# Fewer products, fewer splits and a twelve-part last load in the expert stage of a decoder layer on one Trainium2 core

## The chip, the cores and the metric

The kernel runs on one core of one Trainium2 chip. The metric is device time in microseconds (us) of one execution. Lower is better.

## The reference, cut to what matters

The layer has two parts: a mixer (convolution, sparse attention, retention), which the change leaves alone, and a mixture of 32 experts with top-4 routing over N = 320 tokens of width 1024, in fp32:

```
gate, top_e = softmax(top4(h @ w_router + b_router))       # 4 experts for each token
hu  = x @ w_up[e] + b_up[e]                                # 1024 -> 2048
g   = minimum(hu[:, 0::2], 7.0)
u   = clip(hu[:, 1::2], -7.0, 7.0)
act = (u + 1.0) * g * sigmoid(1.702 * g)
y_e = act @ w_down[e] + b_down[e]                          # 1024 -> 1024
y   = LN(alpha * h + sum_k gate_k * y_k + per_layer_embedding)
```

The 1280 pairs of token and expert make about 40 rows an expert. All weights of all experts are read once: 32 x 12 MB.

## The kernel before, in words

**The stage of the experts.** One *item* is up to 128 rows (slots) of one expert. Item i gathers its rows from `h_dram` (POOL, L1936), turns them (`turn_x`, PE, L536), makes the up product, turns the result back (`turn_hidden`), applies the gated activation, makes the down product and scatters the rows to `y_dram` (POOL, L1942). With these inputs there are 32 items. An item with more than 64 rows is called *many* here (`many_i` holds the flag); there are five, and 27 *few* items.

**Weights.** A weight matrix comes in 1 MB chunks of 128 x 2048: eight for up, four for down, 12 an item (`PER`). SP issues the loads in order (`next_weights`, L465), each into one of six buffers (`chunk_in`) when VectorE has split the chunk that was there (`lo_ready`). The products run in the one-pass fp32r format, so each chunk is split in two: ScalarE writes the rounded part `w_hi` (L1205, waits for the load `w_here` and for `chunk_used`, PE's count of finished chunks), and VectorE writes the rest `w_lo = chunk - w_hi` (L1743, waits for `hi_ready`). Both are rings of three.

**Products.** A *few* item packs its up operand: columns 0:64 of `x_hi` hold the rounded rows and columns 64:128 their rest, so that two passes (`x_hi w_hi`, `x_hi w_lo`) do what a *many* item does in three. `turn_hidden` multiplies with a matrix `turner` that is set for each item (L1758) and adds the two halves for a few item. A many item turns in two halves, and the second waits until VectorE has read the first out of the same two banks (`turned_read`). The down product has three passes for every item: 4 chunks x 3 passes x 4 products = 48.

**Order on PE.** `item(i)`: `turn_hidden(i)`, up product of i+1, `turn_x(i+2)`, down product of i. In ScalarE's and VectorE's order, written out by hand, `part(t)` is one chunk: t = 0 to 7 is the up product of i+1, t = 8 to 11 the down product of i. Between the parts stand, on ScalarE, `result_copy(i-1)` (L1188) after part 2, `squash` (sigmoid, L1192) after 3, `hidden_high` (L1196) after 4, four `hidden_copy` (L1183) after 9, `rows_copy` (L1163) after 10; on VectorE, `hidden_rows` (L1771 to L1791) after part 2, `hidden_product` (L1799) after 3, `hidden_low` (L1806) after 4, `rows_low` (L1755, or L1752 for many) after 9.

**The end.** When the last scatter has landed, SP loads `y_dram` in four transfers (two of 2 MB, two of 512 KB). VectorE then does three token tiles one after the other: four weighted adds (L1871), LayerNorm with `bn_stats` (L1279 to L1282, ScalarE's square root L1014 between), two passes for gain and bias (L1873, L1874); POOL stores each tile (L1966).

Of the kernel before, what the change touches and what calls it, by code (L numbers as in the profile page):

```python
# [20 lines left out]
CAP = 128  # L21
# [124 lines left out]
def build(nc, A, O):  # L146
# [11 lines left out]
    with ctx:  # L158
# [133 lines left out]
        turner, turn_fold, few, many_f = ec.take(HALF), ec.take(HALF), ec.take(NI + 8), ec.take(NI + 8)  # L292
# [13 lines left out]
        y_rows = y_part[:, 0:D]  # L306
        ple = [y_part[:, 0:D], y_part[:, D:2 * D], uu.rearrange("p a b -> p (a b)")]
        y_tok = [arena[:, 0:2 * SLOT], arena[:, 2 * SLOT:4 * SLOT]]
# [28 lines left out]
        up_done, hu_ready, turner_ready = sem("up_done"), sem("hu_ready"), sem("turner_ready")  # L337
        hu_turned, turned_read, g_ready, e_ready, act_ready = sem("hu_turned"), sem("turned_read"), sem("g_ready"), sem("e_ready"), sem("act_ready")
        bias_hi, bias_ready, gates_hi, gates_ready = sem("bias_hi"), sem("bias_ready"), sem("gates_hi"), sem("gates_ready")
        y_stored, var_ready, std_ready = sem("y_stored"), sem("var_ready"), sem("std_ready")  # L340
        y_ready, y_sent, y_here, y_out = sem("y_ready"), sem("y_sent"), many("y_here", 3), sem("y_out")
# [32 lines left out]
        PER = 12  # L374
# [27 lines left out]
        def _(sp):  # L402
# [77 lines left out]
            def next_weights(s, e, c, buf):  # L480

                sp.wait_ge(lo_ready, s + 1)
                weights_to(e, c, buf)

            def first_loads(r):
                s = r * NE * PER
                for t in range(8):
                    e, c = (0, t + 6) if t < 2 else (1, t - 2)
                    next_weights(s + t, e, c, t % 6)

            def item_loads(i, e):
                s = i * PER + 8
                for t in range(PER):
                    of, c = (e + 1, t + 6) if t < 2 else (e, t + 6) if t < 6 else (e + 2, t - 6)
                    next_weights(s + t, of, c, (8 + t) % 6)

            def last_loads(i):
                s = i * PER + 8
                for t in range(6):
                    of, c = (NE - 1, t + 6) if t < 2 else (NE - 2, t + 6)  # L500
                    next_weights(s + t, of, c, (8 + t) % 6)
                for t in range(6, 10):
                    next_weights(s + t, NE - 1, t + 2, (8 + t) % 6)
# [11 lines left out]
            for r in range(1, ROUNDS):  # L515
                with sp.If(n_items > r * NE):
                    for c in range(6):
                        next_weights(r * NE * PER - 6 + c, 0, c, c)
# [4 lines left out]
            rows = y_dram.rearrange("(t k) d -> t (k d)", k=TOPK)  # L523
# [7 lines left out]
        def _(pe):  # L531
# [372 lines left out]
            def turn_half(rhs, inc):  # L904
                for s in range(2):
                    for j in range(8):
                        cols = hu[:, 2 * j * 128 + s:2 * (j + 1) * 128:2]
                        last = mm(psum[:, 6 + s, j * HALF:(j + 1) * HALF], cols, rhs, True, True)
                last.then_inc(hu_turned, inc)

            def turn_hidden(i, many_slots, x_next):
                pe.wait_ge(hu_ready, i * 4 + 4)
                pe.wait_ge(turner_ready, i + 1)
                pe.wait_ge(xlo_ready, x_next)
                with pe.If(many_slots > 0):
                    turn_half(turner, 1)
                    pe.wait_ge(turned_read, i * 2 + 1)
                    turn_half(ident[:, HALF:CAP], 1)
                with pe.If(many_slots < 1):
                    turn_half(turner, 2)  # L920

            def up_product(i, s, many_slots):
# [4 lines left out]
                def product(passes):  # L927
                    for k in range(KT):
                        pe.wait_ge(hi_ready, s + (k + 1))
                        for n_pass, (x, w) in enumerate(passes):  # L930
                            if w is w_lo:
                                pe.wait_ge(lo_ready, s + (k + 1))
# [17 lines left out]
            def down_product(i, s, first):  # L950
                pe.wait_ge(act_hi_ready, i + 1)
                pe.wait_ge(act_lo_ready, i + 1)
                for q in range(4):
                    at = (first + q) % 3
                    pe.wait_ge(hi_ready, s + (q + 1))
                    for n_pass, (x, w) in enumerate(((act_hi, w_hi), (act_lo, w_hi), (act_hi, w_lo))):
                        if w is w_lo:
                            pe.wait_ge(lo_ready, s + (q + 1))
# [1098 lines left out]
```

## Time and profile before

| | |
|---|---|
| median of 3 runs | 1720.52 us (1718.29 to 1721.14) |
| the profiled execution | 1708.54 us, span 1706.7 us |
| granted TensorE clock, mean | 0.916 |
| stage of the experts | from about 490 us to 1650 us of the span |
| after it | 1650 us to 1706.7 us |
| HBM read, mean over the span | 499.43 MB, 292 GB/s moved |

Busy time is in us; "idle before" is the time that the engine sat idle ahead of the instructions of a row and what released it. In a table of windows each row is one stretch of the span.

### The profile page before, as it was taken

The numbers are of one execution on the slowest core, as the hardware profiler recorded it, in microseconds if no ns is written. First come the engines' busy times: TensorE is split into PE (matmuls) and PEld (weight loads), VectorE is DVE, ScalarE is ACT, GpSimd is POOL, SyncE is SP. The second block draws the span as 40 slices with busy tenths as digits, with TensorE's granted clock in tenths as the row PEclk, the third lists the DMA queues.
The fourth block names the chain that finished last, engine by engine and source line by source line (L and its number), as shares of the span: only waits on it lengthen the run. The fifth ranks groups of instructions, "written<-read, shape, count | busy, mean of one in ns | idle before, by whom it ended". The sixth has DMA issues, their size and how long they took to land.

```text
span 1706.7 us, 22653 instructions
## 1 busy us (share of the span) xinstructions
PE 1470.8 (86%) x6949; PEld 1136.5 (67%) x6950; DVE 1289.7 (76%) x1327; ACT 1007.1 (59%) x878; POOL 306.2 (18%) x416
## 2 busy tenths in 40 slices
PE   6983677899989999999999999999998999999950
PEld 4761566554447777777777777777887778778740
DVE  0246564764568899999799999999878997998836
ACT  0111323510147788887688888788756876887620
POOL 5303988800300100010000100100000010000000
PEclk9995787769888999999899999999988999999875
DMA  9984353151348999999799999999977998899742
GB/s 354 359 244 142 91 203 142 28 192 53 134 189 328 350 387 390 384 393 382 261 384 383 390 384 388 384 383 393 362 271 273 389 393 321 327 391 366 272 148 71
DMA packets 123930, 498.52 MB, mean 292 GB/s; under 512 B 20977, under 2 KB 46146, under 8 KB 89618
## 3 DMA queue, kind: packets, MB, share of 16 engines
q1 hardware_dynamic: 103122, 454.56, 70.4%
q0 software_dynamic: 14768, 29.16, 4.9%
q10 hardware_dynamic: 5984, 14.11, 2.4%
q8 instruction: 28, 0.46, 0.1%
q14 instruction: 28, 0.23, 0.0%
HBM read 499.43 MB, written 26.25 MB: 308 GB/s over the span
## 4 chain that ended last, share of the span: by engine, by line
PE 50%; DVE 18%; issue 13%; ACT 8%; SPq 6%; DMA 5%; DVEq 1%; ACTq 0%; POOL 0%; POOLq 0%
PE psum L533 47%; DVE w_lo L1743 9%; ACT w_hi L1205 5%; SPq L388 4%; PE psum L536 3%; DMA arena<-in_w_up 3%; DMA early<-in_pages 1%; DVE arena L1799 1%; DVE arena L1871 1%; DVE arena L1262 1%; DVE arena L1390 1%; DVE arena L1389 1%; DVE arena L1291 1%; ACT arena L1183 1%; SPq L385 1%
## 5 line engine op out<-in xcount | busy, mean ns | idle before, releaser
L1743 DVE TENSOR_TENSOR w_lo<-arena,w_hi 128x2048 fp32r<-128x2048 f32 x384 | 860.9, 2287 | 53.1 <-ACT w_hi L1205 48.8
L1205 ACT ACTIVATE w_hi<-arena 128x2048 fp32r<-128x2048 f32 x376 | 715.3, 1917 | 235.0 <-PE psum L533 234.4
L533 PE MATMUL psum<-w_hi,x_split 128*128 128x512 f32 x2208 | 580.8, 398 | 11.2 <-DVE x_split L1806 6.1
L533 PEld LDWEIGHTS psum<-w_hi,x_split 128*128 128x128 f32 x2208 | 416.8, 191 | 98.7 <-issue 8.5
L533 PE MATMUL psum<-w_lo,x_split 128*128 128x512 f32 x1536 | 432.8, 404 | 49.6 <-DVE w_lo L1743 44.9
L533 PE MATMUL psum<-arena 128*128 128x64 f32 (+10 forms) x2258 | 398.5, 352 | 50.9 <-DMA arena<-in_w_in 17.0
L533 PEld LDWEIGHTS psum<-arena 128*128 128x128 f32 (+4 forms) x2258 | 316.9, 207 | 134.3 <-issue 76.6
L533 PEld LDWEIGHTS psum<-w_lo,x_split 128*128 128x128 f32 x1536 | 282.4, 191 | 155.0 <-DVE w_lo L1743 101.8
L1942 POOL DMA_INDIRECT y_dram<-y_part,arena x32 | 49.9, 1559 | 1044.0 <-ACT y_part L1188 952.4
L536 PE MATMUL psum<-arena 128*128 128x128 f32 (+4 forms) x501 | 80.2, 312 | 66.5 <-ACT arena L1067 28.9
L536 PEld LDWEIGHTS psum<-arena 128*128 128x128 f32 (+4 forms) x501 | 66.0, 158 | 81.3 <-issue 37.3
L1291 DVE TENSOR_REDUCE arena<-early 128x32 f32<-128x2048 f32 x16 | 35.8, 2281 | 109.4 <-DMA early<-in_pages 109.4
L1898 POOL TENSOR_SCALAR arena<-arena,conv_w 128x256 f32<-128x256 f32 (+1 forms) x120 | 84.5, 704 | 11.8
L1899 POOL TENSOR_TENSOR arena<-arena 128x256 f32<-128x256 f32 (+1 forms) x120 | 68.6, 572 | 10.0
L1183 ACT ACTIVATE arena<-psum 128x512 f32<-128x512 f32 x128 | 65.4, 596 | 4.5 <-PE psum L533 3.9
L533 PE MATMUL psum<-early,arena 128*128 128x512 f32 (+1 forms) x152 | 65.5, 634 | 0.0
L1035 ACT ACTIVATE arena<-psum 128x320 f32<-128x320 f32 x23 | 10.1, 437 | 91.2 <-PE psum L533 90.5
L1936 POOL DMA_INDIRECT arena<-h_dram,arena x32 | 39.0, 1219 | 69.2 <-PE psum L536 55.6
L1262 DVE COPY arena<-psum 128x128 f32<-128x128 f32 (+5 forms) x62 | 26.2, 435 | 32.7 <-PE psum L536 21.1
L533 PEld LDWEIGHTS psum<-early,arena 128*128 128x128 f32 (+1 forms) x152 | 25.0, 178 | 37.5 <-issue 37.4
L1755 DVE TENSOR_TENSOR x_split<-psum,x_split 128x512 fp32r<-128x512 f32 x27 | 18.7, 692 | 38.0 <-ACT x_split L1163 36.9
L1019 ACT ACTIVATE arena<-psum 128x512 f32<-128x512 f32 (+6 forms) x32 | 15.9, 517 | 52.0 <-PE psum L536 51.9
(216 smaller groups left out, 758.8 us busy)
## 6 DMA issues: line engine op xcount, KB each, us to landing
arena<-in_w_up SPq DMA_DIRECT2D x256, 1024.0 KB, 7.3
arena<-in_w_down SPq DMA_DIRECT2D x128, 1024.0 KB, 6.9
early<-in_pages SPq DMA_DIRECT2D x160, 128.0 KB, 2.6
arena<-in_w_in ACTq DMA_DIRECT2D x23, 512.0 KB, 7.3
arena<-in_pages POOLq DMA_DIRECT2D x32, 128.0 KB, 7.9
early<-in_pages POOLq DMA_DIRECT2D x32, 128.0 KB, 6.6
arena<-in_pages SPq DMA_DIRECT2D x32, 128.0 KB, 2.2
early<-in_w_plg SPq DMA_DIRECT2D x1, 4096.0 KB, 14.7
```

Of the source, the lines that this page charges most:

```text
L388: eng.dma_start(dst[:, bass.ds(k * 1024 + n * 256, 256)], A["pages"][bass.ds(page, 1), :, part * 256:part * 256 + 256].rearrange("a p n -> ...
L533: return TE.matmul(out, lhsT, rhs, start=start, stop=stop, skip_group_check=True)
L536: return TE.transpose(out, in_, ident[0:in_.shape[0], 0:in_.shape[0]])
L1183: SE.activation(hu[0:CAP, n * 512:n * 512 + 512], psum[0:CAP, n, :], ACT.Copy).then_inc(hu_ready, 1)
L1205: SE.activation(w_hi[:, (8 + t) % 3], chunk_in[(8 + t) % 6], ACT.Copy).then_inc(hi_ready, 1)
L1262: last = VE.tensor_copy(dst, src)
L1291: last = VE.tensor_reduce(cm[:, b, kind].rearrange("p (a b) -> p a b", b=2), cmp_slot[:, b % 2, :, kind].rearrange("p a (b s) -> p a b s", ...
L1743: VE.tensor_tensor(w_lo[:, at], chunk_in[buf], w_hi[:, at].bitcast(f32), SUB).then_inc(lo_ready, 1)
L1898: seen(GE.tensor_scalar(tmp, src(t), conv_w[:, k, t:t + 1], None, MUL))
L1899: seen(GE.tensor_tensor(dst, dst, tmp, ADD))
L1936: pool.indirect_dma_start(out=xg, out_offset=None, in_=h_dram, in_offset=bass.IndirectOffsetOnAxis(ap=slots[:, i, 0:1].bitcast(u32), axis= ...
L1942: pool.indirect_dma_start(out=y_dram, out_offset=bass.IndirectOffsetOnAxis(ap=slots[:, i, 1:2].bitcast(u32), axis=0), in_=y_rows, in_offse ...
```

## The change

Four things change.

1. **Down product of a few item packed.** `hidden_low` writes the rest of the activation into columns 64:128 of `act_hi`, and the product has two passes instead of three. The result stands in two halves of partitions: ScalarE copies the lower half out (`y_low`), and VectorE adds (`result_sum`, new, in VectorE's order after part 2 of the next item). For a many item ScalarE copies the two banks in two instructions. `turner` is gone: a few item turns with a fixed `folder`. The second half of a many item's turn goes to banks 4 and 5, and waits for `y_ready` of the item before instead of `turned_read`. ScalarE branches on `many` too.
2. **The last of the four down chunks is not split.** PE multiplies it straight in fp32 from the load's buffer, 4 products (`act_sb`, `raw`). There are 11 splits an item (`SPLIT`). SP frees that buffer on PE's `chunk_used`, not on `lo_ready`.
3. **Silu.** `act_sb = Silu(1.702 g)` on ScalarE; VectorE then forms `(u + 1) * act_sb` in one instruction, and L1786/L1788/L1791 go. The factor 1.702 is taken out of the gates (`g4`).
4. **The end.** Twelve loads of `y_dram`, one for each tile and choice, each with its own semaphore. The moments are taken on ScalarE (`accum_out`), the order is weigh 0, weigh 1, normalize 0, weigh 2, normalize 1, normalize 2, and a tile's normalization is three VectorE instructions.

```diff
 def next_weights(i, t, e, c, buf, last=False):
+    if t == (3 if last else 11):
+        sp.wait_ge(chunk_used, i * PER + (8 + t + 1 + 3))
+    else:
+        sp.wait_ge(lo_ready, i * SPLIT + (8 + t + 1))
     weights_to(e, c, buf)
...
 def turn_hidden(i, many_slots, x_next, begin):
     with pe.If(many_slots > 0):
+        turn_half(ident[:, 0:HALF], 6).then_inc(hu_turned, 1)
+        if not begin:
+            pe.wait_ge(y_ready, i)
+        turn_half(ident[:, HALF:CAP], 4).then_inc(hu_turned, 1)
     with pe.If(many_slots < 1):
+        turn_half(folder, 6).then_inc(hu_turned, 2)
...
+def down_product(i, first, many_slots):
...
+    def product(passes, rows):
+        for q in range(3):
...
+        pe.wait_ge(w_here[buf], i * 32 + ((first + 3) // 6 * 16 + 16))
+        for a, c in ((0, 0), (0, 1), (1, 0), (1, 1)):
+            last = mm(psum[0:rows, 4 + c, :], act_sb[:, 6 + a, 0:rows], raw[:, a * D + c * 512:a * D + c * 512 + 512], False, a == 1)
         last.then_inc(chunk_used, 1)
+    with pe.If(many_slots > 0):
+        product(((act_hi, w_hi), (act_lo, w_hi), (act_hi, w_lo)), CAP)
+    with pe.If(many_slots < 1):
+        product(((act_hi, w_hi), (act_hi, w_lo)), HALF)
...
 def result_copy(i, used, many_slots):              # ScalarE
+    with act.If(many_slots > 0):
+        SE.activation(y_rows[:, 0:512], psum[:, 4, :], ACT.Copy).then_inc(y_half, 1)
+        SE.activation(y_rows[:, 512:D], psum[:, 5, :], ACT.Copy).then_inc(y_ready, 1)
+    with act.If(many_slots < 1):
+        SE.activation(y_low..., psum[HALF:CAP, 4:6, :], ACT.Copy).then_inc(y_half, 1)
 def squash(i, many_slots):
+    with act.If(many_slots > 0):
+        SE.activation(act_sb, gg, ACT.Silu, scale=SALPHA).then_inc(e_ready, 1)
+    with act.If(many_slots < 1):
+        SE.activation(act_sb[:, :, 0:HALF], gg[:, :, 0:HALF], ACT.Silu, scale=SALPHA).then_inc(e_ready, 1)
...
+def result_sum(i, many_slots):                     # VectorE
+    with dve.If(many_slots < 1):
+        dve.wait_ge(y_half, i + 1)
+        VE.tensor_tensor(y_rows[0:HALF]..., psum[0:HALF, 4:6, :], y_low..., ADD).then_inc(y_ready, 1)
...
-sp.dma_start(y_tok[0], rows[0:128]).then_inc(y_here[0], 16)
-sp.dma_start(y_tok[1], rows[128:256]).then_inc(y_here[1], 16)
-for n in range(2):
-    sp.dma_start(chunk_in[4 + n][0:64], rows[256:320, n * SLOT:(n + 1) * SLOT]).then_inc(y_here[2], 16)
+for m in range(3):
+    for k in range(TOPK):
+        sp.dma_start(y_tok[m][k], rows[m * 128:m * 128 + MT[m], k]).then_inc(y_here[m * TOPK + k], 16)
...
+act.wait_ge(sum_ready, m + 1)                      # ScalarE, for m in range(3)
+SE.activation(spare, acc[0:M, m], ACT.Copy, scale=-1.0 / D, accum_out=mean).then_inc(y_mean, 1)
+SE.activation(spare, acc[0:M, m], ACT.Square, bias=mean, accum_out=y_sq[0:M, m:m + 1]).then_inc(square_ready, 1)
+act.wait_ge(var2_ready, m + 1)
+SE.activation(y_std[0:M, m:m + 1], y_sq[0:M, m:m + 1], ACT.Sqrt).then_inc(std2_ready, 1)
```

VectorE also clears `act_sb` and the upper half of `y_rows` once ahead of the stage, and the set-up of `turn_fold` and `few` is gone.

## Rows read from the trace of the kernel before

**Rows 1.** The page's busy time by engine: busy us, share, instructions.
```profile
PE 1470.8 (86%) x6949; PEld 1136.5 (67%) x6950; DVE 1289.7 (76%) x1327; ACT 1007.1 (59%) x878; POOL 306.2 (18%) x416
```

**Rows 2.** Windows as long as one item: busy by engine, clock, DMA share, GB/s.
```profile
593.15:626.30 33.15, 31.39 (x154) 25.23 (x153) 31.26 (x22) 28.10 (x20) 2.80 (x3) 1.00 1.00 392
...
825.20:858.35 33.15, 28.80 (x134) 24.00 (x133) 24.66 (x22) 18.16 (x12) 2.72 (x2) 0.85 0.70 250
858.35:891.50 33.15, 31.38 (x154) 25.24 (x153) 31.26 (x22) 28.11 (x21) 2.82 (x2) 1.00 1.00 380
...
1488.20:1521.35 33.15, 31.38 (x154) 25.23 (x153) 31.24 (x22) 28.08 (x21) 2.80 (x2) 1.00 1.01 405
```

**Rows 3.** The chain that ended last, in order of time: start, us, what.
```profile
611.24 16.54 PE psum L533 x88
...
644.39 16.54 PE psum L533 x88
...
859.11 16.54 PE psum L533 x88
```

**Rows 4.** Who waited for whom, 560 to 1706 us: total, times, longest.
```profile
ACT w_hi L1205 <- PE psum L533: 226.0, 167, 14.1
...
PE psum L533 <- DVE w_lo L1743: 42.7, 50, 1.2
```

**Rows 5.** The weight loads of L465, 560 to 1600 us, issue to landing.
```profile
DMA to landing us min/median/max: 4.8/7.3/10.9
```

**Rows 6.** VectorE's timeline, one few item: start, duration, instruction.
```profile
681.11 0.69 DVE L1755 TENSOR_TENSOR x_split<-psum,x_split 128x512 fp32r<-128x512 f32 x1 [1.09 <-ACT x_split L1163]
681.72 11.09 DVE L1743 TENSOR_TENSOR w_lo<-arena,w_hi 128x2048 fp32r<-128x2048 f32 x5
692.72 0.69 DVE L1771 TENSOR_TENSOR arena<-psum,arena 128x512 f32<-128x512 f32 x1
...
694.87 0.69 DVE L1791 SCALAR_TENSOR_TENSOR arena<-arena 128x512 f32<-128x512 f32 x1 [0.19 <-DVE arena L1778]
696.04 2.29 DVE L1743 TENSOR_TENSOR w_lo<-arena,w_hi 128x2048 fp32r<-128x2048 f32 x1 [0.48 <-ACT w_hi L1205]
```

**Rows 7.** ScalarE's timeline, the same item.
```profile
694.09 1.92 ACT L1205 ACTIVATE w_hi<-arena 128x2048 fp32r<-128x2048 f32 x1 [2.79 <-PE psum L533]
```

**Rows 8.** PE's timeline around the first many item.
```profile
791.90 2.10 PE L533 MATMUL psum<-w_hi,x_split 128*128 128x512 f32 x8
...
813.80 1.04 PE L536 MATMUL psum<-arena 128*128 128x128 f32 x8
...
825.57 3.87 PE L533 MATMUL psum<-arena 128*128 128x64 f32 x32
831.26 6.85 PE L533 MATMUL psum<-arena 128*128 128x64 f32 x32 [1.82 <-DVE arena L1772]
...
869.86 0.34 PE L533 MATMUL psum<-arena 128*128 128x64 f32 x2
```

**Rows 9.** Windows: fp32 products of 512 columns, and the clock.
```profile
832.00:833.00 1.00, 1.00 (x7) 1.00 (x6) 0.60 (x1) 0.00 (x0) 0.42 (x1) 0.50 0.97 344
841.00:842.00 1.00, 1.00 (x4) 0.81 (x3) 0.00 (x0) 0.34 (x1) 0.00 (x0) 0.59 0.00 0
...
440.00:448.00 8.00, 8.00 (x20) 3.58 (x19) 2.90 (x4) 0.60 (x1) 5.96 (x6) 1.00 0.05 7
```

**Rows 10.** The timeline of the end.
```profile
1649.07 1.02 ACT L1188 ACTIVATE y_part<-psum 128x1024 f32<-128x1024 f32 x1 [6.21 <-PE psum L533]
...
1654.19 0.36 SPq L524 DMA_DIRECT2D arena<-y_dram  x1
...
1655.37 1.28 ACT L1014 ACT_TABLE_LOAD   x1 [5.28 <-issue]
...
1662.37 5.25 DVE L1871 SCALAR_TENSOR_TENSOR arena<-arena 128x1024 f32<-128x1024 f32 x4 [17.18 <-DMA arena<-y_dram]
...
1695.19 0.55 POOL L1966 DMA_DIRECT2D out_y<-arena  x1 [10.19 <-DVE arena L1874]
```

More of the change, by code:

```diff
@@ L291, in build @@
         stats2, mv2, rstd2 = ec.take(2, 6), ec.take(2), ec.take(1)
-        turner, turn_fold, few, many_f = ec.take(HALF), ec.take(HALF), ec.take(NI + 8), ec.take(NI + 8)
+        y_sum, y_mu, y_sq, y_std = ec.take(3), ec.take(3), ec.take(3), ec.take(3)
+        folder, many_f = ec.take(HALF), ec.take(NI + 8)
         ln2 = split(hu, (2, D))
@@ L975, in item @@
                     pe.wait_ge(y_ready, i)
[L976 removed]
+                down_product(i, 16 if end < NE else 8, here)
             def stream(r):
@@ L1183, in hidden_copy @@
                     SE.activation(hu[0:CAP, n * 512:n * 512 + 512], psum[0:CAP, n, :], ACT.Copy).then_inc(hu_ready, 1)
-            def result_copy(i, used):
-                act.wait_ge(chunk_used, used + 3)
-                act.wait_ge(y_sent, i * 16 + 16)
-                SE.activation(y_rows.rearrange("p (c n) -> p c n", c=2), psum[:, 4:6, :], ACT.Copy).then_inc(y_ready, 1)
-            def squash(i):
-                act.wait_ge(g_ready, i + 1)
-                SE.activation(act_sb, gg, ACT.Sigmoid, scale=SALPHA).then_inc(e_ready, 1)
@@ new lines, in squash, with hidden_high @@
+            def squash(i, many_slots):
+                with act.If(many_slots > 0):
+                    act.wait_ge(g_ready, i + 1)
+                    SE.activation(act_sb, gg, ACT.Silu, scale=SALPHA).then_inc(e_ready, 1)
+                with act.If(many_slots < 1):
+                    act.wait_ge(g_ready, i + 1)
+                    SE.activation(act_sb[:, :, 0:HALF], gg[:, :, 0:HALF], ACT.Silu, scale=SALPHA).then_inc(e_ready, 1)
+            def hidden_high(i, many_slots):
+                with act.If(many_slots > 0):
+                    act.wait_ge(act_ready, i + 1)
+                    SE.activation(act_hi, act_sb, ACT.Copy).then_inc(act_hi_ready, 1)
+                with act.If(many_slots < 1):
+                    act.wait_ge(act_ready, i + 1)
+                    SE.activation(act_hi[:, :, 0:HALF], act_sb[:, :, 0:HALF], ACT.Copy).then_inc(act_hi_ready, 1)
@@ L1226, in item @@
                     rows_copy(i + 2)
-                part(11)
             def stream(r):
@@ L1813, in part @@
                 def part(t):
-                    low(s + t, (8 + t) % 3, (8 + t) % 6)
+                    low(i * SPLIT + (8 + t), (8 + t) % 3, (8 + t) % 6)
                 for t in range(3):
                     part(t)
+                if not begin:
+                    result_sum(i - 1, is_many(i - 1))
                 hidden_rows(i, e, here)
@@ L1821, in item @@
                     hidden_low(i, here)
-                    part(3)
+                    result_sum(i, here)
                     return
@@ L1827, in item @@
                 hidden_low(i, here)
-                for t in range(5, 8):
+                for t in range(5, 11):
                     part(t)
-                set_turner(i + 1)
-                part(8)
-                part(9)
                 if end < NE - 1:
                     rows_low(i + 2, is_many(i + 2))
-                part(10)
-                part(11)
             def stream(r):
```

214 lines of the change are left out of this document (115 added, 99 removed).

## The prediction

> **What bounds the kernel now.** I read the page first: PE is busy 86% of the span and VectorE 76% [rows 1]. That is a mean over two different parts, so I cut the experts' stage into windows of one item. In a few item PE is busy 31.4 us of 33.15, VectorE 31.3, ScalarE 28.1, and the DMA engines are at a share of 1.00 with 392 GB/s [rows 2]. Three resources stand within 6% of the period, and the question is which one sets it.
>
> The chain repeats every 33.15 us (611.24 to 644.39) [rows 3], to a few hundredths. Two rows say that this period is VectorE's. ScalarE waited 226.0 us for PE to free `w_hi`, and no wait of it for a load is among the long ones [rows 4]. And after a many item, when all six buffers have had time to fill (share 0.70 in that window), the next item still takes 33.15 us [rows 2, 3]: a kernel bound by its loads would have caught up. VectorE's timeline has hardly a gap in it: five `w_lo` back to back in 11.09 us, 2.22 us each, then the hidden rows; idle are 1.09, 0.19 and 0.48 us [rows 6], which with the 31.3 us busy makes 33.1.
>
> The second row of importance is the share of the DMA engines. When it is 0.70 the rate is 250 GB/s; at 1.00 it is 380 to 405 [rows 2]. The rate divided by the share is 357 to 401, so the share is a fair measure of capacity, and a few item already uses about 99% of it. Its load is 12 MB (12.58 million bytes) and about 0.25 million of gather and scatter: 12.83 million at 390 GB/s are 32.9 us, at 405 they are 31.7.
>
> A many item is bound by PE: its up product alone takes from 791.90 to 813.80, 21.9 us, and its turn 3.87 + 1.82 idle + 6.85, the last at half clock [rows 8, 9]. The two intervals around it last 37.4 and 44.3 us (from 788.1, which is the first product less a turn of 3.87, to 825.57, then to 869.86) [rows 8].
>
> Counting the steady intervals between many items gives 20; the other intervals of the stage touch a many item, its start or its end.
>
> **The change, part by part.**
>
> *VectorE in a few item.* Gone: one `w_lo` (2.22), `turner` (64 columns, an estimate of 0.2, well below the 0.69 of 512 columns), L1791 (0.61 of pitch and 0.19 idle), and the 1.09 of waiting ahead of `rows_low`, because `rows_low` now stands after the last split, in the shadow of the unsplit product [rows 6]. Added: `result_sum`, 1024 columns from PSUM: between 0.69 for 512 columns and 2.29 for 2048, in proportion 1.22 (ends 0.7 and 2.3). Net -2.2-0.8-0.2-1.1+1.2 = -3.1 before new waits.
>
> *PE in a few item.* Down goes from 48 one-pass products to 24 plus 4 in fp32. The 48 take from 814.6 (`turn_x` begins at 813.80 and takes 0.8) to 825.57, 0.228 each [rows 8]. Fp32: 16 products of a turn are recorded as x32 [rows 8], so a product is two records; 20 records of 512 columns filled 8.00 us [rows 9], 0.80 a product. So 24 x 0.228 + 4 x 0.80 = 8.7 instead of 10.9: -2.2. For many it is 36 x 0.228 + 3.2 = 11.4: +0.5.
>
> *ScalarE in a few item.* One `w_hi` less (1.92 [rows 7]), Silu and `hidden_high` on half the columns (512 fewer each, a quarter of 1.92, so -0.45 each): -2.8. It has five us of idle already and decides nothing.
>
> *The new critical loop.* I follow it from the start of the last split, at 0. `w_lo` ends at 2.2; PE's last pass 1.1; the fp32 products 3.2; so the raw chunk is released at 6.6. Only then may ScalarE start the third `w_hi` of the next item (its slot is counted behind that chunk): 8.6. VectorE has done `rows_low` and two splits by 7.6, waits 1.0, then third split 10.8, `result_sum` 12.0, hidden rows 14.0. The fourth `w_hi` needs the turn (3.87) and PE's first chunk (1.8): ready 14.4, so the fourth split ends 16.6; product 17.3, split 19.5, `hidden_low` 20.2, and the last of the next six splits of 2.2, where the loop closes, starts at 31.2. That is the period by compute alone, 31.2; with small new branches and register loads I take 31.6. It is 1.5 below today's, but the loads need 31.7 to 32.9.
>
> *SP.* The raw chunk's buffer comes free 4.4 us later than a split would free it, and two loads queue behind it on SP. With a landing time of 7.3 us at the median [rows 5] and 2.7 us a load, two to three loads are outstanding, so the DMA engines do not run dry in that pause once they are the bound.
>
> (If they did run dry there, the pause of 4.4 us less the 2.7 to 5 that is outstanding would cost up to 1.7 an interval, and the 33.15 of today would come back; that is the last rival.) So steady intervals go from 33.15 to between 31.6 (right after a many item, when buffers are full) and 32.9. The mean I take is 32.5: 20 x 0.65 = **-13**. Ends: 31.6 everywhere, -31; the old 33.15, 0.
>
> *Around many items.* The interval with a many up product and a few down product is PE's: -2.2 each, four of them, -9. The interval with the many turn gains 0.5 for the product and loses about as much in VectorE's shorter rows: 0. The turn's gap stays: `y_ready` now comes after the third split and the sum, 5.5 us after the down product's end, while the first half takes 3.87, so 1.6 to 1.9 us of gap against 1.82 [rows 8], and the fall of the clock to 0.50 until 841.6 [rows 9] stays with it. Only where one many item follows another is no sum in the way, and the gap goes: 1.8, and up to 5 with its stretch of half clock; I take 2. Together **-11** (ends -4 and -16).
>
> *Last item.* From the hidden rows to the last copy: down product -2.2, half-width Silu and `hidden_high` -0.9, L1791 -0.6, sum +1.2: **-2**.
>
> *The end.* Now the first add starts 8.2 us after the issue of the loads (1654.19 to 1662.37), and the three tiles take 32.8 us up to POOL's store at 1695.19 [rows 10]. With a load of 512 KB at about 370 GB/s, 1.4 us each, the first should land after some 3.7 us (its 2 MB forerunner: 8.2, of which 5.6 is transfer). Eight adds of 1.31 are then paced by the landings: 3.7 + 7 x 1.4 + 1.3 = 14.8. Then normalize 0 (variance, wait for Sqrt, reciprocal, two passes of 1.3): 3.3; four adds 5.2; normalize 1, 3.4; normalize 2, with ScalarE's two passes just in time, 3.6: 30.3 against 41.0. **-10** (ends -7 and -12). The extra clears ahead of the stage fall in an idle stretch of VectorE: 0.
>
> Sum: -13 - 11 - 2 - 10 = -36. The profiled execution is 1708.54 us (span 1706.7 and 1.8 around it), 12.0 below the median of 1720.52; I put the difference on the median: 1684.5, **1685 us**.
>
> **Rivals.**
>
> *The table of Silu is loaded in each item.* The trace before has no load in the items' loop, where Copy and Sigmoid alternate; a change of table costs 1.28 us where it occurs [rows 10]. Silu now stands in branches, so what is loaded when they join may be unknown. One load lies between the fourth `w_hi` and Silu and delays the fifth by about 1.0: a compute period of 32.6, which eats what there was after many items: steady 20 x (33.15 - 32.8) = -7, sum -30, 1691. Two loads: 33.9, +15, sum -8, 1713. Centre 1702. Nothing in the rows decides whether it happens.
> "ScalarE activation tables: per-element evaluation and per-set limits" in the Trainium skill (Table sets in the compiler and the runtime) says that the compiler places the loads block by block. "ScalarE: Activation LUTs" (What ACT_TABLE_LOAD costs) adds a drain of about 1.38 us to the 1.28 that the trace shows; by that, an estimate, the loop would be 34.0 us and the result 1715, still not slower.
>
> *The loads are not the bound.* Then 31.6 holds throughout: -31 - 16 - 2 - 12, 1660. For it: 405 GB/s over one item [rows 2]. Against: shares of 1.00 at 380 and 392.
>
> *The clock falls in few items: the case on the other side.* PE will idle some 4 us an item, up to 1.9 at once ahead of the fourth chunk, where VectorE now does the sum as well. Today the longest wait for `w_lo` is 1.2 us [rows 4] at full clock, and after the gap of 1.82 ahead of a turn it fell to 0.50 for ten us [rows 8, 9]. If it falls in each few item, the turn costs 2.98 more and the first chunk 1.8: 31.6 + 4.5 = 36.1, 20 x 3 = +60, 1757. It decides against the change from a steady interval of 34.3 on (23 us spent). Against it: the new gaps stand between products of 512 columns, not beside the turn.
>
> *Nothing gained in steady items* (the new wait for the sum or for the raw chunk gives 33.1 again): only -11 - 2 - 10, 1697.
>
> **How the numbers follow.** Chances: forecast 0.45, no bound by loads 0.12, Silu's tables 0.20, nothing gained when steady 0.13, clock 0.10. The range takes in all but part of the first rival's two-load end, the extreme of the second and the clock: 1662 to 1709. What a measurement can tell from no change is 0.2%, 3.4 us. All cases but the clock and a corner of the tables are faster: faster 0.87, same 0.03, slower 0.10.
>
> **What would show it.** Spacing of steady items 31.6 to 32.9 with the DMA share at 1.00 and ScalarE now waiting for loads; two passes in L533's chunks of the down product and about 3.2 us of fp32 ahead of the turn; no table load between the items; the gap in a many turn still there and one less; the first weighted add some 4 us after the first load's issue and the last store about 30 us after it. Wrong would make it: steady items at 33.1 or above, a granted clock under 1.00 in them, or table loads in the loop.

## The result and the profile after

The changed kernel takes 1742.05 us at the median (8 runs, 1730.35 to 1747.28), the kernel before on the same chip 1720.55 us (8 runs). The ratio is 1.0124 (95% interval 1.0097 to 1.0151): slower by 1.2%, 21.5 us, where 36 us less were forecast. It is above the range, and the profiled execution takes 1745.72 us with a span of 1744.1. One execution of the kernel of experiment 4, of nine, took 2917.53 us, in a slow state, and is left out of its ratio.

The head of the page, busy time of each engine (against [rows 1]):

```profile
span 1744.1 us, 22207 instructions
PE 1473.8 (85%) x6497; PEld 1069.8 (61%) x6498; DVE 1216.5 (70%) x1243; ACT 1024.5 (59%) x930; POOL 290.2 (17%) x416
```

VectorE and PE have less to do, as they should, and the span is longer. So what has grown is the waiting, and the place is found by the groups by line. On ScalarE there are three that the loop did not have before (instructions, then busy us and mean ns of one, then idle us before them):

```profile
L1244 ACT ACT_TABLE_LOAD x31 | 39.8, 1283 | 0.6
L1227 ACT ACT_TABLE_LOAD x27 | 34.6, 1283 | 0.5
L1224 ACT ACT_TABLE_LOAD x5 | 6.4, 1283 | 0.1
```

L1224 and L1227 are Silu in its two branches, L1244 is the `w_hi` behind it, a Copy. Together that is a table load ahead of Silu and another one right behind it, in practically every item. ScalarE's timeline shows them in one item (start, duration, instruction, and in brackets the idle time before it):

```profile
711.11 1.92 ACT L1244 ACTIVATE w_hi<-arena 128x2048 fp32r<-128x2048 f32 x1 [2.86 <-PE psum L537]
713.05 1.28 ACT L1227 ACT_TABLE_LOAD   x1
714.34 0.63 ACT L1227 ACTIVATE arena<-arena 128x512 f32<-128x512 f32 x1
714.99 1.28 ACT L1244 ACT_TABLE_LOAD   x1
716.29 1.91 ACT L1244 ACTIVATE w_hi<-arena 128x2048 fp32r<-128x2048 f32 x1
```

Between the fourth `w_hi` and the fifth there are 3.26 us, of which 2.56 are loads. VectorE and PE are behind it and have nothing else to do. VectorE's timeline, the same item:

```profile
718.23 2.29 DVE L1791 TENSOR_TENSOR w_lo<-arena,w_hi 128x2048 fp32r<-128x2048 f32 x1 [2.27 <-ACT w_hi L1244]
```

and PE's:

```profile
718.25 1.20 PE L537 MATMUL psum<-w_hi,x_split 128*128 128x512 f32 x4 [1.67 <-ACT w_hi L1244]
720.58 2.08 PE L537 MATMUL psum<-w_lo,x_split 128*128 128x512 f32 x4 [1.13 <-DVE w_lo L1791]
722.45 1.72 PE L537 MATMUL psum<-w_hi,x_split 128*128 128x512 f32 x4
```

Four products take 2.08 us instead of 1.08: they run at half clock. The windows of 1 us say so (busy us of PE, PE's weight loads, VectorE, ScalarE, GpSimd; then granted clock, share of the DMA engines, GB/s):

```profile
720.00:721.00 1.00, 0.42 (x1) 0.42 (x2) 1.00 (x2) 1.00 (x2) 0.00 (x0) 0.70 0.85 348
721.00:722.00 1.00, 1.00 (x3) 0.74 (x3) 1.00 (x2) 1.00 (x1) 0.00 (x0) 0.50 0.93 217
722.00:723.00 1.00, 1.00 (x4) 0.78 (x3) 1.00 (x1) 0.63 (x2) 0.00 (x0) 0.50 0.67 197
723.00:724.00 1.00, 1.00 (x4) 0.77 (x3) 1.00 (x2) 1.00 (x1) 0.00 (x0) 0.59 1.01 406
724.00:725.00 1.00, 1.00 (x6) 0.81 (x5) 1.00 (x1) 0.61 (x1) 0.00 (x0) 1.00 1.28 422
```

0.50 is the lower of TensorE's two levels, 1.2 GHz, and it comes after 1.67 and 1.13 us of idle PE with 1.2 us of work between them. The same two gaps do not bring it each time. PE two items earlier, and the window of that item:

```profile
648.94 1.19 PE L537 MATMUL psum<-w_hi,x_split 128*128 128x512 f32 x4 [1.65 <-ACT w_hi L1244]
651.27 1.19 PE L537 MATMUL psum<-w_lo,x_split 128*128 128x512 f32 x4 [1.14 <-DVE w_lo L1791]
```

```profile
631.16:665.71 34.55, 30.33 (x136) 21.51 (x136) 29.46 (x20) 28.21 (x22) 2.21 (x2) 1.00 0.92 344
```

Of the 14 steady items that the chain shows, 3 have a granted clock of 1.00 and take 34.51 to 34.55 us, 7 have 0.95 and take 34.53 to 34.78, 4 have 0.90 or 0.91 and take 35.91 to 36.06. Why the clock falls in some of them and not in others stays open. The chain gives the spacing of the items, against 33.15 in [rows 3]:

```profile
595.10 10.60 PE psum L537 x52
631.16 10.62 PE psum L537 x52
665.71 10.60 PE psum L537 x52
700.49 10.60 PE psum L537 x52
```

36.06, 34.55, 34.78. From 560.37 to 771.17 six of them average 35.13, from 922.08 to 1201.70 eight average 34.95: 35.03 together, 1.88 more than before. With some 20 such intervals that is +38 us. The experts' stage (first `w_hi` to the start of the last scatter) went from 1161.5 to 1194.5 us, +33.0; what follows the last scatter's start from 55.8 to 48.6.

The end came out much as forecast. The issue of the loads (SP) and what follows, against [rows 10]:

```profile
1699.39 6.65 SPq L531 DMA_DIRECT2D arena<-y_dram  x12
```

```profile
1703.65 2.67 DVE L1910 SCALAR_TENSOR_TENSOR arena<-arena 128x1024 f32<-128x1024 f32 x2 [8.88 <-DMA arena<-y_dram]
1716.49 1.28 DVE L1910 SCALAR_TENSOR_TENSOR arena<-arena 128x1024 f32<-128x1024 f32 x1 [2.25 <-DMA arena<-y_dram]
```

```profile
1732.57 0.55 POOL L2028 DMA_DIRECT2D out_y<-arena  x1 [2.55 <-DVE arena L1926]
```

The first add comes 4.26 us after the issue (3.7 forecast) and the last store 33.2 us after it, against 41.0.

### The profile page after: what moved, and what is told of

The parts are those of the page before. It is cut to its first block, busy times and chain, and to the rows that moved or that the text cites. A ratio compares the mean times of both kernels' runs of the same rounds, so it can differ in the third digit from the quotient of the medians.

```text
span 1744.1 us, 22207 instructions
## 1 busy us (share of the span) xinstructions
PE 1473.8 (85%) x6497; PEld 1069.8 (61%) x6498; DVE 1216.5 (70%) x1243; ACT 1024.5 (59%) x930; POOL 290.2 (17%) x416
## 4 chain that ended last, share of the span: by engine, by line
PE 49%; DVE 16%; ACT 13%; issue 12%; SPq 6%; DMA 2%; ACTq 1%; DVEq 0%; POOL 0%; POOLq 0%
PE psum L537 47%; DVE w_lo L1791 9%; ACT w_hi L1244 6%; SPq L391 4%; PE psum L540 2%; ACT arena L1204 2%; ACT L1244 2%; ACT arena L1227 1%; DMA early<-in_pages 1%; DMA arena<-y_dram 1%; DVE arena L1435 1%; DVE arena L1434 1%; DVE arena L1336 1%; SPq L388 0%; ACT arena L1082 0%
## 5 line engine op out<-in xcount | busy, mean ns | idle before, releaser
L1791 DVE TENSOR_TENSOR w_lo<-arena,w_hi 128x2048 fp32r<-128x2048 f32 x352 | 794.6, 2289 | 198.1 <-ACT w_hi L1244 197.4
L1244 ACT ACTIVATE w_hi<-arena 128x2048 fp32r<-128x2048 f32 x344 | 653.1, 1915 | 260.4 <-PE psum L537 259.6
L537 PE MATMUL psum<-arena 128*128 128x64 f32 (+8 forms) x2514 | 521.1, 382 | 47.6 <-DMA arena<-in_w_in 17.0
L537 PE MATMUL psum<-w_hi,x_split 128*128 128x512 f32 x1628 | 462.6, 414 | 53.6 <-ACT w_hi L1244 44.5
L537 PEld LDWEIGHTS psum<-arena 128*128 128x128 f32 (+3 forms) x2514 | 356.8, 205 | 215.2 <-issue 162.8
L537 PE MATMUL psum<-w_lo,x_split 128*128 128x512 f32 x1408 | 419.5, 422 | 53.0 <-DVE w_lo L1791 51.1
L537 PEld LDWEIGHTS psum<-w_hi,x_split 128*128 128x128 f32 x1628 | 318.3, 200 | 132.3 <-ACT w_hi L1244 55.8
L2004 POOL DMA_INDIRECT y_dram<-y_part,arena x32 | 39.0, 1219 | 1092.0 <-DVE y_part L1851 788.1
L540 PEld LDWEIGHTS psum<-arena 128*128 128x128 f32 (+4 forms) x501 | 66.2, 158 | 79.1 <-issue 37.6
L1851 DVE TENSOR_TENSOR y_part<-psum,y_part 64x1024 f32<-64x1024 f32 x27 | 32.6, 1208 | 13.7 <-ACT y_part L1219 13.7
```

The costliest lines, as they stand in the source:

```text
L537: return TE.matmul(out, lhsT, rhs, start=start, stop=stop, skip_group_check=True)
L540: return TE.transpose(out, in_, ident[0:in_.shape[0], 0:in_.shape[0]])
L1244: SE.activation(w_hi[:, (8 + t) % 3], chunk_in[(8 + t) % 6], ACT.Copy).then_inc(hi_ready, 1)
L1791: VE.tensor_tensor(w_lo[:, at], chunk_in[buf], w_hi[:, at].bitcast(f32), SUB).then_inc(lo_ready, 1)
L1851: VE.tensor_tensor(y_rows[0:HALF].rearrange("p (c n) -> p c n", c=2), psum[0:HALF, 4:6, :], y_low.rearrange("p (c n) -> p c n", c=2), ADD) ...
L2004: pool.indirect_dma_start(out=y_dram, out_offset=bass.IndirectOffsetOnAxis(ap=slots[:, i, 1:2].bitcast(u32), axis=0), in_=y_rows, in_offse ...
```

## The experiments

Times of the kernel before beside the experiments are 1718.1 to 1721.0 us. Each ratio is against it.

**1. Sigmoid back, all else as changed.**

```diff
-  SE.activation(act_sb, gg, ACT.Silu, scale=SALPHA)        # in both branches
+  SE.activation(act_sb, gg, ACT.Sigmoid, scale=SALPHA)
+  VE.scalar_tensor_tensor(out=u, in0=u, scalar=1.0, in1=g, op0=ADD, op1=MUL)
-  VE.tensor_scalar(g4, g4, 1.0 / SALPHA, None, MUL)
```

> The changed kernel with one part undone: sigmoid and the multiplication by g on VectorE are back (L1786/L1791 of before), all else as changed, the branches on ScalarE too. Theory T (the two table loads of 1.28 us around Silu delay the fifth w_hi by about 2.6, and the gap of 1.67 + 1.13 us that this opens on PE lets the clock fall to 0.50 for some 3 us): no table load in the items, granted clock near 1.00 in few items, steady items 31.8 to 32.9 us instead of 34.7, time near 1685 to 1695. Rival U (the unsplit chunk or the sum after the third split is what makes the loop longer): steady items stay at 34 or above and the time at 1735 or above. Rival J (the branch alone, without Silu, makes the back end load a table): table loads still there, 2.6 us an item, time as changed or above.

1679.07 us, ratio 0.9758 (0.9745 to 0.9770), below the 1685 to 1695 expected, and no table load between items. The branches are the same: Sigmoid in them needs no load. All of the loss, and 42 us beyond it, goes with Silu.

**2. Silu alone in the kernel before, in straight code** (with what follows from it on VectorE, part 3 of the change).

```diff
-  SE.activation(act_sb, gg, ACT.Sigmoid, scale=SALPHA).then_inc(e_ready, 1)
+  SE.activation(act_sb, gg, ACT.Silu, scale=SALPHA).then_inc(e_ready, 1)
```

> The kernel before with Silu alone: ScalarE's squash is Silu on all columns in straight code, without a branch, and VectorE's L1786 to L1791 go. Theory T-join (loads come from branches, after which the loaded table is not known): no table load in the loop, VectorE 0.8 us shorter, steady items 32.4 to 32.9 instead of 33.15, time 1703 to 1718. Rival S (Silu's table and the one that Copy is given are two, whatever the flow): two loads an item, steady items about 33.15 - 0.8 + 2.3 = 34.7, time near 1755.

1720.18 us, ratio 0.9993 (0.9965 to 1.0020). One load, at the first use of Silu in the whole stage:

```profile
L1192 ACT ACT_TABLE_LOAD x1 | 1.3, 1283 | 0.0
```

So Silu and Copy go together without loads. A second reading: the steady items stay at 33.17 us (chain, 590.74 to 623.91), though L1791 is gone and VectorE is busy for 30.56 us in each instead of 31.26 [rows 2]. VectorE's work did not set the 33.15, and the 1703 to 1718 expected, which rested on it, was missed.

**3. The changed kernel with Silu unbranched.**

```diff
-  with act.If(many_slots > 0):
-      SE.activation(act_sb, gg, ACT.Silu, ...)
-  with act.If(many_slots < 1):
-      SE.activation(act_sb[:, :, 0:HALF], gg[:, :, 0:HALF], ACT.Silu, ...)
+  SE.activation(act_sb, gg, ACT.Silu, scale=SALPHA).then_inc(e_ready, 1)
```

> The changed kernel with Silu on all columns outside of the branch; hidden_high and result_copy keep their branches. T-join: no table load in the items, steady items 31.8 to 32.9, time 1683 to 1695. Rival S: two loads an item as in the changed kernel, time 1740 to 1745.

**1672.72 us, ratio 0.9726 (0.9706 to 0.9746)**: the fastest of all, 48 us below the kernel before and below the 1683 to 1695 expected. Silu takes 1.04 us for all columns instead of 0.63, and yet it is far ahead, because both loads are gone. ScalarE's timeline at the same place in an item:

```profile
637.18 1.92 ACT L1240 ACTIVATE w_hi<-arena 128x2048 fp32r<-128x2048 f32 x1 [2.86 <-PE psum L537]
639.01 1.04 ACT L1223 ACTIVATE arena<-arena 128x1024 f32<-128x1024 f32 x1
639.96 1.90 ACT L1240 ACTIVATE w_hi<-arena 128x2048 fp32r<-128x2048 f32 x1
```

Its windows of two steady items (columns as above):

```profile
594.40:626.56 32.16, 30.00 (x136) 21.59 (x136) 29.46 (x20) 26.70 (x20) 2.19 (x2) 1.00 0.98 384
626.56:658.72 32.16, 29.99 (x137) 21.60 (x137) 29.47 (x20) 26.30 (x20) 2.22 (x2) 1.00 1.01 402
```

The steady items take 32.16 us at full clock, all but one of 33.54 (from 560.86). In that second window the share of the DMA engines is 1.01 at 402 GB/s; before it was 1.00 at 392 [rows 2].

**4. The end alone, in the kernel before** (twelve loads of `y_dram`, moments on ScalarE, the new order; nothing else).

> The kernel before with the end of the change alone (twelve loads, moments on ScalarE, three VectorE instructions a tile). From the changed kernel's trace: first add 4.3 us after the first load's issue, last store 33.2 us after it, against 41.0 before. All theories: 7 to 8 us faster, 1711 to 1714. If the end gained nothing, 1720.

1715.45 us, ratio 0.9968 (0.9944 to 0.9993), 5 us by the medians where 7 to 8 were expected. In its trace the last store is 32.8 us after the issue of the loads, 8.2 less than before.

**5. Packing undone, in the third kernel.**

```diff
-  product(((act_hi, w_hi), (act_hi, w_lo)), HALF)
+  product(((act_hi, w_hi), (act_lo, w_hi), (act_hi, w_lo)), HALF)
# and no result_sum, no y_low; hidden_high on all columns
```

> e3_silu_unbranched with three passes in a few item's down product, no sum on VectorE, one copy out on ScalarE and hidden_high on all columns; the fourth chunk stays unsplit. Theory (PE's down product lies in the loop): 12 products more, 2.7 us, of which part is hidden behind the splits: steady items 33.2 to 34.5, time 1692 to 1715. Rival (VectorE's total work sets the period, and the sum of 1.2 goes): steady items near 31.0 to 32.2, time 1650 to 1673.

1709.14 us, ratio 0.9918 (0.9884 to 0.9951). The chain gives 34.21 us:

```profile
590.42 17.59 PE psum L537 x84
624.63 17.59 PE psum L537 x84
```

VectorE has less to do here than with packing (no sum of 1.21 us), and the item is 2.05 us longer. PE is busy 2.5 us longer in it, for 12 products; ScalarE rounds the activation on twice the columns, some 0.4 us. So most of the 2.05 is PE's down product, and the loop runs through it.

**6. The fourth chunk split again, in the third kernel.**

```diff
-  PER, SPLIT = 12, 11
+  PER, SPLIT = 12, 12
-  for q in range(3):
+  for q in range(4):
-  for a, c in ((0, 0), (0, 1), (1, 0), (1, 1)):    # fp32 from raw
```

> e3_silu_unbranched with the fourth down chunk split like the others (12 splits, part 11 back, two passes for few and three for many). Theory (the loop runs through PE's down product, turn and first up chunk and not through VectorE's sum of work; a split of 2.2 us instead of 3.2 us of fp32 leaves the loop as long): steady items 32.2 to 32.8, time 1673 to 1690. Rival (VectorE's total work sets the period): 32.16 + 2.2 = 34.4, time 1720.

1697.84 us, ratio 0.9882 (0.9816 to 0.9947), 25 us above the third kernel and above the 1673 to 1690 expected. Where the clock holds the item is even shorter: 31.81 us where the third kernel has 32.04 at the same place behind a many item, and 31.97 for the next (to 956.70) against 32.16, with VectorE busy nearly all the time; VectorE's timeline, one item apart:

```profile
892.92 2.29 DVE L1782 TENSOR_TENSOR w_lo<-arena,w_hi 128x2048 fp32r<-128x2048 f32 x1 [1.46 <-ACT w_hi L1233]
924.73 2.29 DVE L1782 TENSOR_TENSOR w_lo<-arena,w_hi 128x2048 fp32r<-128x2048 f32 x1
```

But the clock does not hold everywhere. Windows of 100 us:

```profile
600.00:700.00 100.00, 91.40 (x399) 71.22 (x398) 91.50 (x60) 80.31 (x60) 8.29 (x6) 0.91 0.95 372
900.00:1000.00 100.00, 89.30 (x422) 68.40 (x422) 98.44 (x63) 86.69 (x63) 11.42 (x6) 1.00 0.99 397
```

So the unsplit chunk does not pay by a shorter loop. What goes with the 25 us is the clock: with that chunk every steady item of the third kernel's trace is at 1.00, and without it, of five in a row from 588.32 on, one stands at 0.90 (34.69 us), two at 0.86 (36.08 and 35.91 us) and two at 1.00 (32.0 us). Why it falls there was not tested.

**7. Branches around Silu, in the second kernel,** and the load of `many` into a register that they need. Both branches do the full columns, so that the work is the same.

```diff
-  SE.activation(act_sb, gg, ACT.Silu, ...)
+  with act.If(many_slots > 0):  SE.activation(act_sb, gg, ACT.Silu, ...)
+  with act.If(many_slots < 1):  SE.activation(act_sb, gg, ACT.Silu, ...)
```

> e2_silu_alone (no loads in the loop, steady items 33.17 us, 1720 us) with Silu put into a branch on many, on all columns either way, and nothing else. T-join (after a branch the loaded table is not known, so Silu and the Copy behind it each get a load): two loads an item, steady items 35.3 to 36.0, time 1765 to 1785. Rival (the loads of the changed kernel needed its other branches, of hidden_high and result_copy, too): no loads, 1720.

1798.85 us, ratio 1.0461 (1.0402 to 1.0521), above what either theory gave; the steady items take 36.1 us on average of 13, a little above the 36.0 expected, and where the rest of the excess lies stays open. The loads are there again:

```profile
L1210 ACT ACT_TABLE_LOAD x31 | 39.8, 1283 | 0.6
L1197 ACT ACT_TABLE_LOAD x27 | 34.6, 1283 | 0.5
L1194 ACT ACT_TABLE_LOAD x5 | 6.4, 1283 | 0.1
```

It takes Silu and the branch together: Silu in straight code has no loads (experiment 2), and Sigmoid in branches has none either (experiment 1). They are as many, 32 and 31, as in the changed kernel. Why the compiler gives them to Silu and not to Sigmoid stays open.

**8. Loads in place without a branch, in the third kernel.**

```diff
+  SE.activation(y_std[0:1, 0:1], many_f[0:1, 0:1], ACT.Sqrt)        # one element, ahead of Silu
   SE.activation(act_sb, gg, ACT.Silu, scale=SALPHA)
```

> e3_silu_unbranched with a Sqrt on one element right ahead of Silu, so that the same two loads stand where the changed kernel has them, without a branch. If the loads at that place are the whole loss: steady items 34.7 to 35.5, clock falling to 0.50 for some 3 us in many of the few items, time 1735 to 1755. Rival (the branch itself costs, in fetching or in its waits): steady items near 33, time under 1715.

1766.87 us, ratio 1.0285 (1.0236 to 1.0334), above the 1735 to 1755 expected. Sqrt and Silu each load a table (2 x 1.28, and 0.2 for the element); steady items take 36.41 and 35.28 us in turn, 35.83 on average of six (chain, 559.79 to 774.79). Two loads alone, put back at this place, turn the fastest kernel into one slower than before.

**9. Copies in place of the loads.** Six copies of one element ahead of Silu and six behind it, no load.

> The kernel with Silu unbranched, and six Copy of one element (about 1.1 us) ahead of Silu and six behind it, where the changed kernel has its two loads of 1.28 us, with no load here. Theory A, a load costs just the time for which it keeps ScalarE from its work, at a place on the loop: 2.2 us of delay give steady items of 34.0 to 34.6 where the clock is full, the clock falls after the gaps as with the loads, and the time is 1725 to 1765. Theory B, a load costs more than its 1.28 us (something it does to the tables, the queues or the transfers): then copies of nearly the same length cost clearly less, 1675 to 1715.

1703.70 us, ratio 0.9915 (0.9894 to 0.9936). That fits the second theory's range, but for another reason: I had the copies too long. Six of them take 0.64 us and overlap with Silu, 1.1 us of delay in all. The steady item takes 33.23 us (chain, 581.95 to 748.12, five items), 1.07 more than without them, at a granted clock of 1.00. The price of a delay at this place is one for one.

**10. Longer copies in place.** Four copies of 128 columns and four of one element, each time.

> The kernel with Silu unbranched, and ahead of Silu and behind it four Copy of 128 columns and four of one element, an estimate of 1.3 us each time (twelve single elements took only 1.1 us in all), so about as long as the two loads of 1.28 us, at the same places. With 1.1 us of delay the steady items went from 32.16 to 33.23 us at full clock. Theory A, a load costs only its time, and the clock falls by the gap on PE that comes of it, whatever made the gap: steady items of 34.5 to 34.7 where the clock is full, mean clock under 1.00 in windows of steady items, 1730 to 1765. Theory B, the fall of the clock or a part of the time belongs to the load itself: steady items at or below 34.6 with the clock at 1.00 throughout, 1705 to 1725.

1822.69 us, ratio 1.0617 (1.0571 to 1.0663). Now they came out longer than estimated, 2.0 us each time, so the time is above what either theory gave; the item takes 37.47 us, 5.31 more, and the clock falls with no table load in any steady item. The chain, and a window of that item:

```profile
638.07 10.60 PE psum L537 x52
675.54 10.62 PE psum L537 x52
```

```profile
638.07:675.54 37.47, 32.09 (x136) 23.51 (x136) 29.64 (x20) 29.95 (x36) 2.22 (x2) 0.91 0.86 332
```

Set side by side: from the start of the fourth `w_hi` to that of the fifth ScalarE takes 2.78 us in the third kernel, 3.88 in experiment 9, 5.18 in the changed kernel, 5.70 in experiment 8 and 7.06 here. The delay against the third kernel and what the item grew by on average are then 1.10 and 1.07 (copies), 2.40 and 2.87 (the changed kernel), 2.92 and 3.67 (Sqrt ahead), 4.28 and 5.31 (copies). Loads and copies lie on one curve. In the changed kernel's items whose clock stayed at 1.00 (34.55 us) the growth is 2.39, so a load costs the time that it takes. What comes on top, 0.47 to 1.03 us an item, stands in traces in which the granted clock of some or all steady items is 0.90 to 0.95.

**11 to 14. Loads and copies in ScalarE's slack,** behind `rows_copy(i + 2)`, in the third kernel: one element each of Sqrt and Silu (two loads), then Copy in their place, then twelve copies, then sixteen longer ones.

```diff
                   rows_copy(i + 2)
+              SE.activation(y_std[0:1, 0:1], many_f[0:1, 0:1], ACT.Sqrt)
+              SE.activation(y_std[0:1, 1:2], many_f[0:1, 0:1], ACT.Silu)
```

> e3_silu_unbranched (steady items 32.16 us, 1673 us) with a Sqrt and a Silu on one element added after rows_copy, so that two tables are loaded in each item where ScalarE has about 2.5 us of idle time before PE frees the third slot. If the place decides what a load costs: steady items 32.2 to 32.9, clock 1.00 in few items, time 1675 to 1692. Rival (two loads cost their 2.57 us wherever they stand): steady items 34.7, time 1725 to 1740.

> e5_loads_in_slack with Copy in place of Sqrt and Silu on the one element, so that the two small instructions stay and no table is loaded. e5 lost 150 us because every other gather (POOL, out of h_dram) took 17 us instead of 1 and PE waited for its rows. If the table loads bring that about, directly or by shifting VectorE's work by 2.6 us against POOL: no long gathers here, steady items 32.2 to 32.6, time 1673 to 1685. If the small instructions or the place do: long gathers again, time near 1820.

> The kernel with Silu unbranched, and twelve Copy of one element (about 0.18 us each, some 2.3 us) in ScalarE's slack behind the rows of the item after next, where an earlier kernel had two loads of tables (2.9 us with the two small instructions). That one took 1824.8 us, and in 11 of 32 items the gather of the rows took 17.1 us instead of 1.0. Theory A, the loads themselves hold up the gather: here no gather is long (mean about 1.1 us) and the time is 1672 to 1680. Theory B, the delay of ScalarE by some 2.5 us moves the gather to where it collides with something: gathers of 17 us appear here too, and the time is above 1750.

> The same sixteen copies, about 2.6 us together, in ScalarE's slack behind the rows of the item after next, where two loads of tables brought 1824.8 us and gathers of 17.1 us in 11 of 32 items. Twelve copies of one element there took only some 1.3 us and left the gathers alone. Theory A, the loads hold up the gather: no long gather, 1674 to 1690. Theory B, a delay of ScalarE of this length brings the gather to a bad place: gathers of 17 us and over 1750.

1824.75 us with the two loads (ratio 1.0598, 1.0536 to 1.0661), 1675.60 with two copies (0.9749, 0.9710 to 0.9788), 1677.65 with twelve (0.9767, 0.9714 to 0.9819), 1848.57 with sixteen longer ones, 4.1 us together (1.0765, 1.0717 to 1.0813). The first was a surprise: a pause in the slack was to cost next to nothing, and even the rival gave only 1725 to 1740. Its loss is not on ScalarE. It is a gather of POOL, which issues the rows of the item after next:

```profile
L1996 POOL DMA_INDIRECT arena<-h_dram,arena x32 | 211.5, 6610 | 69.8 <-PE psum L540 56.2 <-issue 8.8 <-DMA arena<-slot_dram 4.9
```

A mean of 6.6 us against 1.1 in the third kernel, and in 11 of the 32 items 17.1; PE waited for these rows 11 times, 126.0 us in all. The twelve copies left every gather short, as if the loads were to blame, but they last only 1.2 us together. The long copies, with no load in the slack, give the same 211.5 us of busy POOL, 11 long gathers and 127.9 us of PE waiting; so it is the delay, not the table. The trace of the sixteen copies shows what is different in an item with a long gather. POOL:

```profile
619.31 1.01 POOL L2000 DMA_INDIRECT arena<-h_dram,arena  x1 [0.30 <-issue]
653.75 17.10 POOL L2000 DMA_INDIRECT arena<-h_dram,arena  x1 [0.31 <-issue]
```

and VectorE around the two:

```profile
619.42 2.29 DVE L1793 TENSOR_TENSOR w_lo<-arena,w_hi 128x2048 fp32r<-128x2048 f32 x1 [0.54 <-ACT w_hi L1240]
...
658.86 11.09 DVE L1793 TENSOR_TENSOR w_lo<-arena,w_hi 128x2048 fp32r<-128x2048 f32 x5
670.48 2.29 DVE L1793 TENSOR_TENSOR w_lo<-arena,w_hi 128x2048 fp32r<-128x2048 f32 x1 [0.53 <-ACT w_hi L1240]
```

The short gather begins in VectorE's idle half microsecond (618.88 to 619.42). The long one finds none: VectorE runs without a gap from 643.64 to 669.95, and the gather ends at 670.85, 0.9 us after the first gap. With the two loads in the slack it is the same (no gap from 639.21 to 665.51, gather from 649.32 to 666.42). "SBUF — State Buffer" in the Trainium skill (SBUF: two separate sides) describes this: GpSimd cannot write the descriptors of a transfer that it issues while VectorE holds the port pair that they share. These rows agree with it in time. The trace of experiment 6 does not fit as well: there a gather from 925.12 takes 2.80 us, though VectorE has no gap from 924.73 to 941.44, and none of its gathers is longer than 2.94. So a missing gap alone does not make a long gather; no run here gave VectorE a gap on purpose, and as a cause the lock is argued, not shown.

## Why the prediction was wrong

**The step that failed is the first rival: its chance and its price.** The forecast's sum has no term for table loads, and says of ScalarE that it "has five us of idle already and decides nothing". The text had the mechanism as a rival, "what is loaded when they join may be unknown", and gave it 0.20 because nothing in the rows decided it. Experiments 1, 2, 3 and 7 settle it: Silu in straight code is loaded once, Silu in a branch brings two loads in each item, and without that branch the change is worth 48 us. In the sum, the steady items were to give -13 and came out at +38. And ScalarE does decide between the fourth `w_hi` and the fifth: 1.10 us of copies there lengthen the item by 1.07 (experiment 9), whatever idle time it has elsewhere. What the trace of before did show was that a function whose table is loaded already needs no load; that held for Sigmoid in the branches and not for Silu.

**Its price was short by the base and by the clock.** Two loads were put at a period of 33.9 and a total of 1713. Measured are 34.55 where PE's clock holds and 35.03 on average, 1742. Of the 1.13 us that the period lacked, 0.56 are the loop without loads (31.6 for 32.16), 0.09 the delay (2.3 for 2.39) and 0.48 the clock. The text worked out a table rival and a clock rival, each by itself, and the second followed on the first: the delay opens the gaps of 1.67 and 1.13 us, and the clock fell in 11 of the 14 steady items, though not in all that have the gaps. The clock rival's bound, "decides against the change from a steady interval of 34.3 on", was crossed by the loads alone; it had counted on 23 us from the other parts, and they gave 12. (Its 31.6 + 4.5 was a slip as well: 2.98 and 1.8 are 4.8.) Experiment 10 shows the fall with no load in the steady items.

By the page "ScalarE: Activation LUTs" of the Trainium skill (What ACT_TABLE_LOAD costs) a drain of 1.38 us comes on top of each load. No such gap is in this trace: the load at 714.99 takes 1.28 and the next instruction starts at 716.29, and the one at 713.05 starts 0.02 after `w_hi` ends. The estimate of 34.0 us and 1715 made with it, "still not slower", counts one load; with two, which is what came, the same working gives 33.9 + 2 x 1.38 = 36.7, above the 35.03 measured.

**"This period is VectorE's" was wrong.** Experiment 2 takes 0.7 us from VectorE at no change; experiment 5 takes the sum off it and loses 2.05. That the loop ran PE's down product, the turn, the fourth `w_hi`, and only then VectorE's splits is shown for the third kernel by experiments 5 and 9; for the kernel before it is read from its chain, in which 16.54 of the 33.15 us are PE's [rows 3]. The 32.9 us as a floor of the loads was wrong as well: the third kernel runs at 32.16 with the share at 0.98 to 1.01, and experiment 6 at 31.81. The share reads 1.00 at 392 GB/s before and 1.01 at 402 in the third kernel, so it did not measure what was left. The mean of 32.5 came out near 32.16 although one of the ideas behind it fell.

**What held, on the third kernel, which has no loads.** The loop walked gave 31.2, taken as 31.6, against 32.16. It had the wait of VectorE for the fourth `w_hi` (0.4, measured 0.55). It had the third split starting 8.6 us after the last one where the trace has 9.1 (624.22 to 633.31), and no wait ahead of the next last split where the trace has 0.53. The sum takes 1.21 (1.22 forecast), the fp32 products about 3.4 (3.2), packing 2.05 us an item by experiment 5 (2.2 forecast for packing and the unsplit chunk together, on PE). The experts' stage is 36.9 us shorter than before (26 forecast: -13 steady, -11 around the many items, -2 at the last): 20 intervals of 0.99 less make 20 of them, 17 lie around the many items and the last. The end is 7.8 us shorter in the changed kernel (10 forecast, ends 7 and 12), with two waits for landings, 0.78 and 2.25 us, between the adds; in the third kernel the last store is 31.4 us after the issue, 9.6 less than before. One gap of a many item less: PE waited for `result_sum` 4 times, at most 1.6 us:

```profile
PE psum L537 <- DVE y_part L1851: 6.2, 4, 1.6
```

Without the table loads the forecast of 1685 would have been 12 us too high, with the right sign. With them, the changed kernel's accounts are: stage +33.0 (20 x 1.88 = +38 steady, some -5 elsewhere), end -7.2, which is +25.8 in the profiled executions and +21.5 by the medians. The profiled execution before entered the stage 11.6 us earlier than the one after (489.4 and 501.0), in code that the change leaves alone. The forecast put this difference on the median instead, and rightly so: the kernel of experiment 2 enters the stage at 501.1 as well.

## What to carry to other kernels

Silu in a branch was given two table loads an item, and in straight code one for the whole stage. So look for table loads within the loop by line, and if a branch around a ScalarE function brings them, do the full width in both cases rather than the half in one. Where ScalarE, VectorE and PE work on each other's results in a ring, find the loop by what each waits for and by taking work away, not by which engine is busiest. A delay on it cost one for one here while PE's clock stayed full, and more where it fell. A pair of rivals in which one sets off the other has to be priced together.

## What the runs showed of the hardware that was not expected

- Copy, which had followed Sigmoid without a load all the time, was given a load of 1.28 us after each branch that held Silu (31 of them at L1244); Sigmoid in the same branches brought none.
- A pause of 4.1 us in ScalarE's slack, or two table loads, 3.0 us with their elements, costs 152 to 176 us in all and goes with 11 gathers of 17.1 us; one of 1.2 us costs 5 us by the medians, within the spread of the third kernel's runs (1668.14 to 1680.39). ScalarE's idle time alone does not tell which delay is harmless.
- The granted clock fell to 0.50 after idle stretches of 1.67 and 1.13 us on PE, neither of them as long as the 1.82 us ahead of the turn in [rows 8], and stayed at 1.00 after 1.65 and 1.14 us in another item of the same trace.
- With the fourth chunk split, PE does not have its 3.4 us of fp32 work ahead of the turn, a steady item takes 0.2 us less where the clock holds, and the kernel 25 us more, with a clock that falls to 0.86 over whole items. That the fp32 work holds the clock up was not tested.
